# Five of the seven half-size products of a gated FFN tile: high part and rest of the moving operand through one weight load

## The reference

```python
D_MODEL = 1024; SEQ = 512; D_FF = 2816
def swiglu(h, w_gate, w_up, w_down):
    return (jax.nn.silu(h @ w_gate) * (h @ w_up)) @ w_down
...
x = x + 0.5 * swiglu(rms_norm(x, ffn1_norm[i]), ffn1_w_gate[i], ffn1_w_up[i], ffn1_w_down[i])
...
def swiglu_2(hn, w_in, w_out):
    gu = hn @ w_in
    return (jax.nn.silu(gu[..., :FFN_HIDDEN]) * gu[..., FFN_HIDDEN:]) @ w_out
```

## Time and profile before

| | us |
|---|---|
| runs | 2514.51, 2512.61, 2514.9 |
| median | 2514.51 |
| profiled execution, first to last instruction | 2514.8 |
| TensorE busy in it | 2457.7 |
| VectorE busy in it | 1726.5 |

### The profile page before, as it was taken

One profiled execution on the slowest core, in us unless ns is written; L12 is line 12 of the kernel. 1 busy time (PEld: TensorE's weight loads), 2 busy tenths in 40 slices (PEclk: granted clock), 3 DMA queues, 4 the chain that ended last, 5 costly groups with the idle time before them and its releaser, 6 DMA issues.

```text
span 2514.8 us, 37950 instructions
## 1 busy us (share of the span) xinstructions
PE 2457.7 (98%) x15202; PEld 2108.7 (84%) x15202; DVE 1726.5 (69%) x2551; ACT 1252.5 (50%) x1799; POOL 1358.7 (54%) x672
## 2 busy tenths in 40 slices
PE   8999999999999999999999999999999999999999
PEld 6899987777789999777887889999877777999987
DVE  5777752888677777586666687776687567777755
ACT  5333343568553433567555553333455685343343
POOL 4677754232457777446544357777444224777754
PEclk9999999999999999999999999999999999999999
DMA  4333333111223333222211133333332113333333
GB/s 142 101 101 101 102 113 113 59 59 55 88 89 105 105 102 104 84 76 84 60 35 35 44 100 101 101 101 109 92 92 84 51 34 101 101 101 101 101 102 124
DMA packets 61790, 223.64 MB, mean 89 GB/s; under 512 B 6704, under 2 KB 6832, under 8 KB 61488
## 3 DMA queue, kind: packets, MB, share of 16 engines
q1 hardware_dynamic: 60928, 218.07, 27.5%
q10 hardware_dynamic: 688, 3.15, 0.3%
HBM read 219.10 MB, written 2.10 MB: 88 GB/s over the span
## 4 chain that ended last, share of the span: by engine, by line
PE 78%; DVE 12%; ACT 6%; issue 3%; DMA 1%; POOL 0%; SPq 0%; DVEq 0%; ACTq 0%
PE ps L661 6%; PE ps L662 6%; PE ps L663 6%; PE ps L586 5%; PE ps L588 5%; PE ps L587 5%; PE ps L578 4%; PE ps L577 4%; PE ps L576 4%; PE ps L1799 2%; PE ps L998 2%; PE ps L1800 2%; PE ps L1801 2%; PE ps L1000 2%; PE ps L999 2%
## 5 line engine op out<-in xcount | busy, mean ns | idle before, releaser
L2970 POOL TENSOR_TENSOR w_lo<-raw,w_hi 128x1024 fp32r<-128x1024 f32 (+1 forms) x405 | 942.3, 2337 | 975.5 <-ACT w_hi L496 974.2
L496 ACT ACTIVATE w_hi<-raw 128x1024 fp32r<-128x1024 f32 (+1 forms) x405 | 397.1, 983 | 661.2 <-PE ps L578 432.2
L2977 POOL TENSOR_TENSOR t_lo<-t_sum,t_hi 128x1024 fp32r<-128x1024 f32 x140 | 336.2, 2423 | 50.2 <-DVE t_sum L773 40.9
L661 PE MATMUL ps<-mid_hi,w_hi 128*128 128x512 f32 x704 | 275.4, 391 | 6.6 <-DVE h L887 3.4
L662 PE MATMUL ps<-mid_lo,w_hi 128*128 128x512 f32 x704 | 274.8, 390 | 0.0
L663 PE MATMUL ps<-mid_hi,w_lo 128*128 128x512 f32 x704 | 273.9, 389 | 0.0
L586 PE MATMUL ps<-sx_hi,t_hi 128*128 128x256 f32 x840 | 238.3, 284 | 5.9 <-DVE ff_up L840 5.9
L588 PE MATMUL ps<-sx_hi,t_lo 128*128 128x256 f32 x840 | 238.0, 283 | 0.0
L587 PE MATMUL ps<-sx_lo,t_hi 128*128 128x256 f32 x840 | 238.0, 283 | 0.0
L887 DVE SCALAR_TENSOR_TENSOR h<-ps,h 128x512 f32<-128x512 f32 x320 | 200.5, 683 | 35.3 <-PE ps L663 25.0
L501 ACT ACTIVATE t_hi<-t_sum 128x1024 fp32r<-128x1024 f32 x140 | 148.0, 1061 | 93.3 <-DVE t_sum L771 51.0
(11 more groups left out here) (455 smaller groups left out, 6456.3 us busy)
## 6 DMA issues: line engine op xcount, KB each, us to landing
raw<-in_units_dram SPq DMA_DIRECT2D x406, 512.0 KB, 3.6
...
```

Of the source, the lines that this page charges most:

```text
L496: nc.scalar.activation(w_hi[:, n % W_SLOTS, begin:], raw[:, n % RAW_SLOTS, begin:], ACT.Copy).then_inc(s_whi, 1)
L661: nc.tensor.matmul(out, hi, mid_hi[:, mid, :], start=(k == 0), stop=False)
L2970: nc.gpsimd.tensor_tensor(w_lo[:, n % W_SLOTS, begin:], raw[:, n % RAW_SLOTS, begin:], w_hi[:, n % W_SLOTS, begin:].bitcast(F32), ALU.subt ...
L2977: nc.gpsimd.tensor_tensor(t_lo[x % 2][part][:, :, :], t_sum[x % 2][part][:, :, :], t_hi[x % 2][:, 2 * part:2 * part + 2, :].bitcast(F32), ...
```

## The change

A matmul of 256 columns by x high part and one of 256 columns by the rest use the same weights. In products 1, 2, 4, 5 and 6 they become one matmul of 512 columns: its moving operand is two pieces of 256 columns (high part and rest), for which `x_hi` and `x_lo`, and the two parts of `sx_hi` and `sx_lo`, are placed in one tensor each (`x_hl`, `sx_hl`). It writes two halves of a PSUM bank, the second of which now holds the sum over the rest. Products 3 and 7 (bank c) keep their three matmuls, since the other half of that bank holds d. The halves are added by VectorE: the copy p1 becomes a `tensor_reduce` over the two halves, u2 and u3 take a second addition each, and product 5 no longer accumulates on product 1, so that a takes two additions (e1 = a + p1, a = second half + e1), as e does. The sums of x lie in two tensors, so that one addition over 1024 columns becomes two over 512.

```diff
-        x_hi = place("x_hi", 56 * KB, [P, DK, T], F32R)
-        x_lo = place("x_lo", 72 * KB, [P, DK, T], F32R)
+        x_hl = place("x_hl", 56 * KB, [P, 2, DK, T], F32R)
+        x_hi, x_lo = x_hl[:, 0, :, :], x_hl[:, 1, :, :]
...
-        sx_sum = place("sx_sum", M + 32 * KB, [P, 4, 4, HT])
-        sx_lo = place("sx_lo", M + 32 * KB, [P, 4, 4, HT], F32R)
-        sx_hi = [place(f"sx_hi{i}", at + 16 * KB, [P, 2, 4, HT], F32R) for i, at in enumerate((MID_HI, MID_LO))]
+        sx_step = (2 * 4 * HT, 6 * KB)
+        sx_hl = [place(f"sx_hl{i}", at, [P, 2, sx_step[i]], F32R) for i, at in enumerate((M + 32 * KB, MID_HI + 16 * KB))]
+        sx_sum = [place(f"sx_sum{i}", at, [P, 2, 4, HT]) for i, at in enumerate((M + 40 * KB, MID_LO + 16 * KB))]
...
         def pe_strassen(pe, w, x, n, gate_free, second_free, up_free, g, pair, lent_bank, first):
 
-            a, b, c = ps[:, 4 * g + 2 * pair, 0:HT], ps[:, 4 * g + 2 * pair + 1, 0:HT], ps[:, lent_bank, 0:HT]
             gate, up, r = n % W_SLOTS, (n + 1) % W_SLOTS, x % 2
-
-            def product(out, slot, at, moving, start, done):
+            a, b, c = 4 * g + 2 * pair, 4 * g + 2 * pair + 1, lent_bank
+
+            def both(bank, hi, lo, moving, start, stop):
+
+                out = ps[:, bank, :].rearrange("p (a t) -> p a t", a=2)
+                nc.tensor.matmul(out, hi, moving, start=start, stop=False, skip_group_check=True)
+                return nc.tensor.matmul(ps[:, bank, 0:HT], lo, moving[:, 0, :], start=False, stop=stop, skip_group_check=True)
+
+            def single(bank, hi, lo, moving, start, stop):
+
+                out = ps[:, bank, 0:HT]
+                nc.tensor.matmul(out, hi, moving[:, 0, :], start=start, stop=False, skip_group_check=True)
+                nc.tensor.matmul(out, hi, moving[:, 1, :], start=False, stop=False, skip_group_check=True)
+                return nc.tensor.matmul(out, lo, moving[:, 0, :], start=False, stop=stop, skip_group_check=True)
+
+            def product(bank, passes, slot, at, moving, start, done):
                 for k in range(4):
                     cols = slice((at + k) * P, (at + k + 1) * P)
-                    hi, lo = w_hi[:, slot, cols], w_lo[:, slot, cols]
-                    m_hi, m_lo = moving(k)
-                    nc.tensor.matmul(out, hi, m_hi, start=(start and k == 0), stop=False, skip_group_check=True)
-                    nc.tensor.matmul(out, hi, m_lo, start=False, stop=False, skip_group_check=True)
-                    last = nc.tensor.matmul(out, lo, m_hi, start=False, stop=(k == 3), skip_group_check=True)
+                    last = passes(bank, w_hi[:, slot, cols], w_lo[:, slot, cols], moving(k), start and k == 0, k == 3)
                 last.then_inc(done, 1)
 
-            def sum_product(out, i, moving, start):
+            def sum_product(bank, passes, i, moving, start):
                 for k in range(4):
                     cols = slice(k * P, (k + 1) * P)
-                    hi, lo = t_hi[r][:, i, cols], t_lo[r][i // 2][:, i % 2, cols]
-                    m_hi, m_lo = moving(k)
-                    nc.tensor.matmul(out, hi, m_hi, start=(start and k == 0), stop=False, skip_group_check=True)
-                    nc.tensor.matmul(out, hi, m_lo, start=False, stop=False, skip_group_check=True)
-                    last = nc.tensor.matmul(out, lo, m_hi, start=False, stop=(k == 3), skip_group_check=True)
+                    last = passes(bank, t_hi[r][:, i, cols], t_lo[r][i // 2][:, i % 2, cols], moving(k), start and k == 0, k == 3)
                 last.then_inc(s_prd, 1)
 
             def plain(k0, begin):
-                return lambda k: (x_hi[:, k0 + k, begin:begin + HT], x_lo[:, k0 + k, begin:begin + HT])
+                return lambda k: x_hl[:, :, k0 + k, begin:begin + HT]
 
             def summed(i):
-                return lambda k: (sx_hi[k // 2][:, k % 2, i, :], sx_lo[:, k, i, :])
+                return lambda k: sx_hl[k // 2][:, :, (k % 2 * 4 + i) * HT:(k % 2 * 4 + i + 1) * HT]
 
             pe.wait_ge(s_wlo, n + 1)
             pe.wait_ge(s_free, gate_free)
-            product(a, gate, 0, plain(0, 0), True, s_prd)
+            product(a, both, gate, 0, plain(0, 0), True, s_prd)
             pe.wait_ge(s_tlo, 2 * x + 1)
             pe.wait_ge(s_free, second_free)
             if first:
-                pe.wait_ge(s_xsum, 15 * w.ffn + 15)
-            sum_product(b, 1, summed(1), True)
+                pe.wait_ge(s_xsum, 16 * w.ffn + 16)
+            sum_product(b, both, 1, summed(1), True)
             pe.wait_ge(s_free, up_free)
-            sum_product(c, 0, summed(0), True)
+            sum_product(c, single, 0, summed(0), True)
             pe.wait_ge(s_tlo, 2 * x + 2)
-            pe.wait_ge(s_sv, 7 * x + 2)
-            sum_product(b, 2, summed(2), False)
-            product(a, gate, 4, plain(4, 0), False, s_used)
-            pe.wait_ge(s_sv, 7 * x + 3)
-            sum_product(b, 3, plain(4, HT), False)
+            pe.wait_ge(s_sv, 12 * x + 3)
+            sum_product(b, both, 2, summed(2), False)
+            product(a, both, gate, 4, plain(4, 0), True, s_used)
+            pe.wait_ge(s_sv, 12 * x + 5)
+            sum_product(b, both, 3, plain(4, HT), False)
             pe.wait_ge(s_wlo, n + 2)
-            pe.wait_ge(s_sv, 7 * x + 4)
-            product(c, up, 4, summed(3), False, s_used)
+            pe.wait_ge(s_sv, 12 * x + 6)
+            product(c, single, up, 4, summed(3), False, s_used)
...
-                dve.wait_ge(s_xsum, 15 * f + 8)
-                nc.vector.tensor_tensor(sx_sum[:, :, 1, :], sx_sum[:, :, 0, :], x_part[:, 0:8:2, :], ALU.subtract).then_inc(s_xsum, 1)
-                dve.wait_ge(s_xsum, 15 * f + 9)
+                dve.wait_ge(s_xsum, 16 * f + 8)
+                for i in range(2):
+                    nc.vector.tensor_tensor(sx_sum[i][:, :, 1, :], sx_sum[i][:, :, 0, :], x_part[:, 4 * i:4 * i + 4:2, :], ALU.subtract).then_inc(s_xsum, 1)
...
                 x = S_OF[n]
                 gate, up = ps[:, 4 * g + 2 * pair, :], ps[:, up_bank(g, t), :]
-                a, b = gate[:, 0:HT], ps[:, 4 * g + 2 * pair + 1, 0:HT]
-                c, d, e = up[:, 0:HT], up[:, HT:T], gate[:, HT:T]
-                p1, u2, u3 = ff_gate[:, pair, 0:HT], ff_up[:, pair, 0:HT], ff_up[:, pair, HT:T]
+                second = ps[:, 4 * g + 2 * pair + 1, :]
+                a, a2, b, b2 = gate[:, 0:HT], gate[:, HT:T], second[:, 0:HT], second[:, HT:T]
+                c, d = up[:, 0:HT], up[:, HT:T]
+                p1, e1, u2, u3 = ff_gate[:, pair, 0:HT], ff_gate[:, pair, HT:T], ff_up[:, pair, 0:HT], ff_up[:, pair, HT:T]
                 dve.wait_ge(s_prd, 5 * x + 1)
-                nc.vector.tensor_copy(p1, a).then_inc(s_sv, 1)
+                nc.vector.tensor_reduce(p1, gate.rearrange("p (a t) -> p t a", a=2), AX.X, ALU.add).then_inc(s_sv, 1)
                 dve.wait_ge(s_prd, 5 * x + 2)
-                dve.wait_ge(s_sv, 7 * x + 1)
+                dve.wait_ge(s_sv, 12 * x + 1)
                 nc.vector.tensor_tensor(u2, b, p1, ALU.add).then_inc(s_sv, 1)
+                dve.wait_ge(s_sv, 12 * x + 2)
+                nc.vector.tensor_tensor(u2, b2, u2, ALU.add).then_inc(s_sv, 1)
                 dve.wait_ge(s_prd, 5 * x + 4)
                 nc.vector.tensor_tensor(u3, b, p1, ALU.add).then_inc(s_sv, 1)
-                dve.wait_ge(s_sv, 7 * x + 3)
+                dve.wait_ge(s_sv, 12 * x + 4)
+                nc.vector.tensor_tensor(u3, b2, u3, ALU.add).then_inc(s_sv, 1)
+                dve.wait_ge(s_sv, 12 * x + 5)
                 nc.vector.tensor_tensor(d, c, u3, ALU.add).then_inc(s_sv, 1)
                 if t + 1 in picked:
                     dve_weight_sums(dve, x + 1)
+                dve.wait_ge(s_used, n + 1)
+                nc.vector.tensor_tensor(e1, a, p1, ALU.add).then_inc(s_sv, 1)
+                dve.wait_ge(s_sv, 12 * x + 7)
+                nc.vector.tensor_tensor(a, a2, e1, ALU.add).then_inc(s_sv, 1)
+                dve.wait_ge(s_sv, 12 * x + 8)
                 dve.wait_ge(s_prd, 5 * x + 5)
-                nc.vector.tensor_tensor(e, b, p1, ALU.add).then_inc(s_sv, 1)
-                dve.wait_ge(s_sv, 7 * x + 5)
+                nc.vector.tensor_tensor(e1, b, p1, ALU.add).then_inc(s_sv, 1)
+                dve.wait_ge(s_sv, 12 * x + 9)
+                nc.vector.tensor_tensor(a2, b2, e1, ALU.add).then_inc(s_sv, 1)
+                dve.wait_ge(s_sv, 12 * x + 10)
                 nc.vector.tensor_tensor(ff_gate[:, pair, :], gate, rstd[:, :], ALU.mult).then_inc(s_free, 1)
...
```

More of the change, by code:

```diff
@@ L696, in act_x_sum @@
         def act_x_sum(act, w, i):
-                act.wait_ge(s_xsum, 15 * w.ffn + 9 + 2 * i + 2)
-                nc.scalar.activation(sx_hi[i][:, :, :, :].rearrange("p a b t -> p (a b t)"),
-                                     sx_sum[:, 2 * i:2 * i + 2, :, :].rearrange("p a b t -> p (a b t)"), ACT.Copy).then_inc(s_xpart, 1)
+                act.wait_ge(s_xsum, 16 * w.ffn + 10 + 2 * i + 2)
```

(21 more changed lines are left out.)

## The result

| | changed kernel | kernel before |
|---|---|---|
| median, us | 2593.83 | 2514.66 |
| lowest, us | 2591.82 | 2512.61 |
| profiled execution, us | 2590.0 | 2514.8 |
| ratio to before, 95% interval | 1.0315, 1.03 to 1.0329 | |

The account below looks back on a forecast made before the run. TensorE bounds the kernel before; after the change VectorE sets the repeat. 2514.8 + 78.5 (66 repeats) + 2.8 (first tiles) - 0.4 (plain tiles) = 2595.7 us, said as 2596; range 2553 to 2637, 8 in 10.

Parts of the forecast that it names:

- the new bound: VectorE's chain from u3 to u2's second addition holds up product 4; repeat 16.73 instead of 15.54 us, 66 times.
- the 0.05 for a second wait: On VectorE, a step with two waits costs 0.05 us more, at u2 and at the second b + p1.
- the reduce, taken as 0.69: VectorE's tensor_reduce replacing the copy p1: 0.69 us, 0.28 more than the copy, bounds 0.41 and 1.24.
- the meeting with GpSimd: GpSimd's w_lo runs between second and third weight sums, 2.54 to 3.70 us after u3; the fourth ends at 4.96.
- the rival: GpSimd's w_lo after all four weight sums, a + p1 1.09 us sooner; alone: repeat 15.64, 2524 us, chance 0.05.
- The first tiles: Each FFN's first Strassen tile, where u2 was late already: 0.69 us more, four times, 2.8 us.
- TensorE's gain: Merged matmuls in five products save 0.24 us a Strassen tile, 16.8 us in 70 tiles.
- the pair's price: On TensorE, a 512-column matmul at 0.228 us replaces two of 256 at 0.120 each, saving 0.012.
- the first rival: VectorE keeps up: GpSimd's turn after the weight sums and overlapping additions; TensorE bounds, 2498 us, chance 0.07.
- Waits of 95 us: Product 4's first matmul waits for u2's second addition, some 1.4 us in each of 66 repeats.
- the second rival: GpSimd's turn alone comes later, after the four weight sums: repeat 15.64 us, 2524 us, chance 0.05.
- That the additions overlap: Rival: VectorE's dependent additions follow each other at 0.34 instead of 0.46 us; 2556 us, chance 0.10.

Follow-up runs that it names:

- e3_three_matmuls: Changed kernel with each merged matmul again two of 256 columns, both with the start flag, so part of the computation is dropped; 2593.55 us, ratio 1.0316.
- e2_te_alone: Changed kernel's merged matmuls with VectorE's instructions of the kernel before, one sum left out of five products; 2503.91 us, ratio 0.9957 to the kernel before.
- e5_copy: Changed kernel with the reduce replaced by the earlier copy of a's first half, the rest part left out of p1; 2574.26 us, ratio 1.0243.
- e4_pool_late: Changed kernel with one more wait on GpSimd, so the half-size w_lo starts only after the four weight sums; 2518.75 us, ratio 1.002.

## Why the prediction was right

**The bound and its place.** Right. The forecast put the new bound on VectorE's chain from u3 to the second addition of u2, with product 4 as the one who waits; e3_three_matmuls shows it from the one side (16.72 without any merged matmul) and e2_te_alone from the other (15.40 without the additions).

**The chain.** Forecast and measured times after u3: a + p1 4.88 and 4.89, the gate's product with rstd 6.77 and 6.73, the reduce 13.24 and 13.20, u2 14.03 and 13.99, its second addition 14.49 and 14.45, the next u3 16.73 and 16.69. The 0.04 is b + p1 for e (L864), which starts 0.47 after the step before it and not 0.51: the 0.05 for a second wait, read from the one row of 745.47, is there before u2 (0.11 behind the reduce's end) and not here. Term by term:
- the reduce, taken as 0.69 between bounds 0.41 and 1.24, is 0.68, and e5_copy shows that its surcharge counts in full. The Trainium skill, VectorE: DVE Perf Modes, Rules for kernel authors, expects one element per cycle and calls it the slowest operation; the trace doesn't show the second, for the reduce takes 0.68 where an elementwise step over 512 elements takes 0.69 (L868).
- the meeting with GpSimd went as the earlier trace rows told: w_lo between the second and the third sum. e4_pool_late shows that it was worth 16.69 - 15.59 = 1.10 us a repeat; 1.09 stood in the rival.
- from the end of the second addition to u3: 264.50 - 262.68 = 1.82, forecast 1.81.

**The sum.** 66 x 1.15 = 75.9 us by the traces, where 78.5 were forecast. The first tiles were mis-sized too: TensorE's waits for u2 there are 7.3 us in all, 1.4 more than before, where 2.8 stood. The profiled executions differ by 75.2 us, so 2590.0 stands against the 2595.7 of the sum. The medians differ by 79.2: the profiled execution was the fastest of the changed kernel (2591.82; the next two 2593.48 and 2594.18), and its span is 1.8 us shorter than its time, where before the change span and median were 0.3 apart. That 2596 lies so near the median is in part luck: two terms were some 4 us too large, and the scatter of the executions covers it.

**TensorE's gain.** Mis-sized: 16.8 us forecast, 10 measured. The term that was wrong is the pair's price, 0.228 + 0.120, taken from matmuls that stand among their like. It did no harm, since that gain lies under VectorE's chain. It would have, had the forecast been the first rival: its 2498 would have been 2504. The figure of the Trainium skill, TensorE: Matmul & The Clock Gate, Back-to-back issue gap, 2.5 ns a pair and 3.5 us in all by the estimate from it, is too small by about as much as mine was too large: 7.6 ns a pair were measured.

**The profile to come.** Waits of 95 us were announced, 80.0 are booked. The lateness itself was 1.27 us at the start and 0.07 in the first matmul where 1.43 stood; the rest is the booking from the modelled end. 512 and 256 columns came at 236 and 117 ns, not 228 and 120. TensorE's busy share is 95%, not 94%.

**The rivals.** The first, VectorE keeps up, needed two things at once that did not happen. One of them, GpSimd's turn after the sums, can be had by a single wait in the code, and gives 2518.75, near the 2524 of the second rival. That the additions overlap is refuted by every 0.46 in the timeline.
